# Stick-breaking heads moved into the groups of the other heads of attention 3, and two chunks of the gated linear mixer prepared beside them

## The chip, the cores and the metric

One core of a Trainium2 chip runs the whole program. The metric is the device time in microseconds (us) of one execution, the median of three. The engines are named as in the profile: PE is TensorE, DVE is VectorE, ACT is ScalarE, POOL is GpSimd, and SP issues most DMAs. All data are 32-bit floats. Each matmul instruction of the program stands as two records in the trace, so "x2" behind a matmul row is one instruction.

## The reference, cut to what matters

The program runs three layers on 512 tokens of width 1024. The first two are attention layers with weights of their own and do not change. The third projects its input once and mixes the tokens in three ways, whose outputs are gated, joined and projected back:

```python
# six "NSA" heads, each with three softmax branches: cmp (compressed keys), sel, win
o = gate0 * o_cmp + gate1 * o_sel + gate2 * o_win
# four stick-breaking heads (sb): no softmax, a cumulative sum from the last key back
z = (q @ k.T) * scale                           # keys strictly before the query
log_a = log_sigmoid(z) + reverse_cumsum(log_sigmoid(-z))[next key]
o_sb = exp(log_a) @ v
# six HGRN2 heads (hg): linear attention with a decaying state, in chunks
b = cumsum(log_f);  att = (q * k * exp(b_t - b_s)) summed, causal
o_hg = att @ v + (q * exp(b)) @ state
out = layer_norm(ALPHA * x + concat(o_nsa * silu(z1), o_sb * silu(z2), o_hg * silu(z3)) @ w_out)
```

Tokens are handled in four query tiles of 128 (index i or t, 0 to 3). A tile i sees keys 0 to 128(i+1), so its score rows are 128, 256, 384 or 512 wide; those of the branch cmp are 7, 15, 23 or 31 wide.

## The kernel before

The work around the change is "attention 3", the attention of the third layer, and the mixer stage that follows it, which I call the tail.

**Units.** Attention 3 has 88 units (72 NSA, 16 stick-breaking), each one head of one branch on one query tile, numbered 0 to 87 here in the order of `attention_plan`. Units form groups that share one PSUM bank OB and are closed together: 12 groups of six NSA units (cmp, sel, win of tile 0, then of tile 1, and so on), and then four groups of four stick-breaking units, units 72 to 87. Every engine walks the same list, one step per unit (`steps`). In step r

- PE issues the scores (L919, into SC) of units up to two ahead. For the NSA kinds they come in pairs, at even steps, and the two of a pair have their 64 rows of keys in different halves of the array, because `row_halves` orders heads 0, 3, 1, 4, 2, 5. Then come some filler matmuls (L867), the transposes of unit r's weights (L934, into PT), more fillers, and the products with the values (L897, into OB) of unit r-1.
- DVE first does the cmp mask product of unit r (`finish_weights`, L1677), then masks the new scores (L2023 for NSA, which also finds the row maximum; L1677 for sb), and then what is left over: gates, the closing of the group that ended two steps ago (`finish_group`), and one piece of each open chain.
- ACT does the exponential of each new score row (L1367), a piece of each open chain, copies the transposed weights out of PSUM (L1208, pts<-PT), and then what belongs to finished filler tiles.

**A stick-breaking unit** costs more: DVE adds the mask (L1677), ACT takes abs, exp and log (L1361 to L1363), DVE does a sum, a reversed scan and another sum (L1685, L1975, L1685; `stick_tail`), and ACT a last exp (L1339). Before, its z stands in zm, which has two buffers shared with the other units.

**Fillers.** 25 tiles of input projections (FILLERS[2], eight matmuls each: nz, sbq, sbk, sbvz, hf, hz, hq, hi) are spread over the steps by SPREAD[2]: before, 21 tiles over 68 steps and four over 14 more, so two or three matmuls in each of the steps 0 to 81. A tile `hf` starts a chain of three pieces on DVE and two on ACT (`forget_tile`), one piece a step; its second DVE piece holds the reciprocal of L1893.

**The tail** needs, for each 128-token chunk c, operands made by POOL and ACT: `differences(c)` on POOL, `exponentials(c)` on ACT (L1396 to L1401), `operands(c)` on POOL. Before, POOL starts when the last NSA unit is done and the first stick unit masked, and ACT's part is done inside steps 78 and 84. PE starts the tail when the last group is closed and chunk 0's operands are there; chunk 1's are needed one chunk later. The tail goes on through four chunks, the output projection (L960) and the layer norm.

**Weights** come through a ring of three slots of 2 MB (`ring_slots`), each loaded when the last user of its slot is done.

## Time and profile before

| | us |
|---|---|
| median of three runs (1392.6 to 1395.92) | 1394.83 |
| the profiled execution, whole | 1397.89 |
| its span, first to last instruction | 1396.4 |
| attention 3, first unit to the tail (947.3 to 1256.4) | 309.1 |
| the tail (1256.4 to 1396.4) | 140.0 |
| PE busy over the span | 1232.1 (88%) |
| mean granted clock of PE | 0.917 |

A timeline row gives the start, the length, the engine, the line, what is written from what, the shape, the count, and in brackets how long the engine was idle before it and what ended that. The granted clock is a share of 2.4 GHz; 0.60 in a stretch means that PE ran most of it at 1.2 GHz.

### The profile page before, as it was taken

What the parts mean: (1) busy time and instruction counts of PE and PEld (TensorE: products, weight loads), DVE (VectorE), ACT (ScalarE), POOL (GpSimd) and SP (SyncE); (2) the same over time, 40 slices, a digit from 0 to 9 for tenths busy, and PEclk for the clock granted to TensorE, in tenths of its full rate; (3) what the DMA queues carried; (4) which work ended last, traced back from release to release, by engine and by line L of the source; (5) the groups of instructions that cost most, each with busy time, mean ns of one, the idle gap of its engine ahead of it and who ended that gap; (6) DMA issues with size and microseconds to landing.
All of it is one profiled execution on the core that took longest, in us unless ns stands there. A gap on an engine that the chain in (4) does not pass through costs nothing.

```text
span 1396.4 us, 15111 instructions
## 1 busy us (share of the span) xinstructions
PE 1232.1 (88%) x5264; PEld 687.7 (49%) x5264; DVE 553.4 (40%) x1422; ACT 427.5 (31%) x1086; POOL 112.6 (8%) x140
## 2 busy tenths in 40 slices
PE   4879986999897899889999989999999899867974
PEld 1555453455564444334455555555454556545541
...
GB/s 348 100 91 31 91 121 177 151 211 151 1 1 1 121 61 37 49 97 61 61 61 61 1 0 124 54 186 34 30 36 46 46 61 61 1 0 32 1 31 30
DMA packets 60258, 99.71 MB, mean 71 GB/s; under 512 B 12068, under 2 KB 22129, under 8 KB 60184
## 3 DMA queue, kind: packets, MB, share of 16 engines
...
## 4 chain that ended last, share of the span: by engine, by line
PE 73%; DVE 14%; ACT 6%; DMA 3%; issue 2%; ACTq 1%; POOL 0%; DVEq 0%; SPq 0%; POOLq 0%
PE PR L867 32%; PE OB L897 6%; PE PT L779 6%; PE SC L919 6%; PE PR L779 5%; PE OB L779 4%; PE SC L779 4%; PE PT L934 3%; DMA ring<-in_w_ada 3%; DVE stage L1677 2%; PE PR L960 2%; DVE d L1677 1%; DVE tok L1677 1%; DVE arena L1893 1%; PE PR L851 1%
## 5 line engine op out<-in xcount | busy, mean ns | idle before, releaser
L867 PE MATMUL PR<-ring,hT 128*128 128x512 f32 (+1 forms) x784 | 382.2, 600 | 4.4 <-ACT hT L1208 3.5
L867 PEld LDWEIGHTS PR<-ring,hT 128*128 128x128 f32 x784 | 137.9, 200 | 105.2 <-issue 88.2
L1367 ACT ACTIVATE stage<-stage,nmax 128x256 f32<-128x256 f32 (+7 forms) x200 | 103.7, 519 | 261.3 <-DVE nmax L2023 230.0
L897 PEld LDWEIGHTS OB<-arena,pts 128*128 128x128 f32 (+3 forms) x880 | 132.9, 202 | 99.0 <-issue 76.5
L867 PE MATMUL PR<-hT,ring 128*128 128x512 f32 (+1 forms) x304 | 150.7, 619 | 0.0
L1585 POOL TENSOR_TENSOR arena<-arena 128x192 f32<-128x192 f32 (+1 forms) x118 | 80.4, 681 | 798.0 <-PE OB L897 749.2
L897 PE MATMUL OB<-arena,pts 128*128 128x64 f32 (+4 forms) x880 | 131.0, 278 | 11.4 <-ACT pts L1208 11.4
L919 PE MATMUL SC<-arena 64*128 64x256 f32 (+15 forms) x432 | 114.4, 455 | 10.2 <-DVE nmax L2023 10.2
L934 PEld LDWEIGHTS PT<-ident,stage 128*128 128x128 f32 (+3 forms) x440 | 59.7, 148 | 108.2 <-issue 70.1
L1208 ACT ACTIVATE pts<-PT 128x256 f32<-128x256 f32 (+7 forms) x200 | 80.9, 404 | 95.2 <-PE PT L934 72.8
L934 PE MATMUL PT<-ident,stage 128*128 128x128 f32 (+3 forms) x440 | 88.1, 292 | 20.9 <-ACT stage L1339 11.8
L2023 DVE CUSTOM_DVE_ANT_0 stage<-SC,causal 128x128 f32<-128x128 f32 (+3 forms) x96 | 47.1, 491 | 105.5 <-issue 55.5
L867 PEld LDWEIGHTS PR<-hT,ring 128*128 128x128 f32 (+1 forms) x304 | 51.1, 190 | 52.4 <-issue 51.2
L960 PE MATMUL PR<-ring,hT 128*128 128x512 f32 x128 | 61.3, 632 | 6.1 <-DVE hT L2232 6.1
L2023 DVE CUSTOM_DVE_ANT_0 stage<-SC,arena 128x128 f32<-128x128 f32 (+7 forms) x72 | 27.9, 388 | 81.5 <-PE SC L919 79.8
L919 PEld LDWEIGHTS SC<-arena 64*128 64x128 f32 (+2 forms) x432 | 46.7, 192 | 21.3 <-DVE nmax L2023 10.6
L779 PE MATMUL PR<-ring,hT 128*128 128x512 f32 (+5 forms) x160 | 50.2, 470 | 3.9 <-ACT hT L1251 2.0
L1681 DVE TENSOR_SCALAR t<-PR 128x512 f32<-128x512 f32 (+3 forms) x29 | 17.4, 599 | 87.1 <-PE PR L867 76.2
L779 PE MATMUL SC<-ring,hT 128*128 128x512 f32 (+3 forms) x144 | 51.4, 516 | 0.0
L779 PE MATMUL PT<-ring,hT 128*128 128x512 f32 (+4 forms) x144 | 50.0, 502 | 0.0
L960 PEld LDWEIGHTS PR<-ring,hT 128*128 128x128 f32 x128 | 25.1, 204 | 34.8 <-issue 28.2
L779 PEld LDWEIGHTS PR<-ring,hT 128*128 128x128 f32 x160 | 28.1, 200 | 22.8 <-issue 16.6
...
## 6 DMA issues: line engine op xcount, KB each, us to landing
...
ring<-in_od_w_in SPq DMA_DIRECT2D x8, 2048.0 KB, 14.4
...
ring<-in_ev_w_out SPq DMA_DIRECT2D x2, 2048.0 KB, 10.2
...
```

The costliest lines, as they stand in the source:

```text
L779: mm = pe.matmul(dst, lhs(k), rhs(k), start=(k == 0), stop=(k == K - 1))
L867: mm = pe.matmul(dst, l, r, start=(k == 0), stop=(k == KT - 1))
L897: mm = pe.matmul(ob[:, h * w:h * w + w], pts[0:rows_, v % 2, n * P:n * P + P], vb, start=(n == 0), stop=(n == len(blocks) - 1))
L919: pe.matmul(SC[s % 2][:, 0:n], q, k, start=True, stop=True).then_inc(s_done, 1)
L934: tr = pe.transpose(PT[v % 2][0:w, b * P:b * P + P], pb[:, s % NP, b * P:b * P + w], ident[:, :])
L960: mm = pe.matmul(b[:, :], hT[:, k, i * P:i * P + P], W[:, k, :], start=(k == 0), stop=(k == KT - 1))
L1208: return act.activation(dst, src, ACT.Copy, scale=scale)
L1367: give(act.activation(pb[:, s % NP, 0:n], zm[:, s % 2, 0:n], ACT.Exp, bias=nmax[:, row, c:c + 1], scale=-1.0, accum_out=rsum[:, row, c:c + ...
L1585: return pool.tensor_tensor(dst, a, b, op)
L1677: return dve.tensor_tensor(dst, a, b, op)
L1681: return dve.tensor_scalar(dst, a, s1, None, op0)
L2023: give(dve.tensor_tensor_reduce(out=z, in0=SC[s % 2][:, 0:n], in1=mask, scale=-scale, scalar=start, op0=ALU.add, op1=ALU.min, accum_out=nm ...
```

## The change

- The stick-breaking units no longer form groups of their own. Two of them (heads h and h+1 of tile t) are put into each of eight NSA groups, win of tile 0 to cmp of tile 3 (STICKS), as third and sixth unit of what is then a group of eight. Their products go to columns 384 to 511 of the group's OB, and `finish_group` multiplies them into tok with one more DVE operation.
- "sb" is now among the kinds whose scores are issued in pairs. So a stick unit's scores are paired with those of an NSA unit.
- z and its logs have one buffer each (sbz, sbl) instead of zm and t1/t2, and a semaphore of their own, sb_p. The mask of one stick unit therefore waits for the last exp of the one before. The DVE tail of a stick unit and its last exp are done one step after its mask, behind the copy of the transposed weights on ACT.
- SPREAD[2] is new: 11 tiles over 11 steps (eight matmuls a step), nine over 33 steps (two or three), three over 22 and two over 22 (one or none). The hf tiles end at steps 14, 18 and 21 (before 38, 41 and 44), the last tile at step 87.
- The slot of nz is kept as room for the operands of chunk 0, so that hf, hz, hq, hi and the output weights alternate between the other two slots. POOL makes chunk 0's differences as soon as the three hf chains are done, and chunk 1's when the last stick unit is done (unit 73). ACT's exponentials are cut into three pieces, one a step, behind steps 34 and 79. The rest of the tail's buffers moves within the arena.

The diff, cut to its core:

```diff
-SPREAD = [..., [(21, 68), (4, 14)]]
+SPREAD = [..., [(11, 11), (9, 33), (3, 22), (2, 22)]]
-SIDE_BY_SIDE = ("swa", "cmp", "sel", "win")
+SIDE_BY_SIDE = ("swa", "cmp", "sel", "win", "sb")
+STICKS = dict(zip([(0, "win"), (1, "cmp"), (1, "sel"), (1, "win"), (2, "cmp"), (2, "sel"), (2, "win"), (3, "cmp")],
+                  [(t, h) for t in range(T) for h in (0, 2)]))
...
-            groups += [(kind, i, [[(kind, h, i)] for h in row_halves(NSH)]) for kind in ("cmp", "sel", "win")]
-        groups += [("sb", i, [[("sb", h, i)] for h in range(SBH)]) for i in range(T)]
+            for kind in ("cmp", "sel", "win"):
+                units = [[(kind, h, i)] for h in row_halves(NSH)]
+                if (i, kind) in STICKS:
+                    t, h = STICKS[i, kind]
+                    units[2:2] = [[("sb", h, t)]]
+                    units[5:5] = [[("sb", h + 1, t)]]
+                groups.append((kind, i, units))
...
-HG_EARLY = (78, 84)
+EXP_STEPS = (34, 79)
...
+        sbl = spare[:, 3456:3968]
+        sbz = arena[:, 17088:17600]
...
# ACT, in the loop over the steps
                         if su[0] == "sb":
-                            t = (t1, t2)[s % 2][:, 0:n]
...
-                            stick_tail()
-                            pending.append(s)
+                            link(act.activation(sbl[:, 0:n], sbz[:, 0:n], ACT.Abs))
+                            link(act.activation(sbl[:, 0:n], sbl[:, 0:n], ACT.Exp, scale=-1.0))
+                            say(act.activation(sbl[:, 0:n], sbl[:, 0:n], ACT.Ln, bias=1.0), sb_l, "sb_l")
+                            sticks.append((r_, s))
                             continue
...
                     give(copy(pts[0:r, v % 2, 0:w], PT[v % 2][0:r, 0:w]), pt_ev[v % 2], v // 2 + 1)
+                    if sticks and sticks[0][0] < r_:
+                        stick_tail(sticks.pop(0)[1])
...
-                    if L == 2 and r_ in HG_EARLY:
-                        exponentials(HG_EARLY.index(r_))
+                    if L == 2 and r_ in EXP_STEPS:
+                        chains.append(exponentials(EXP_STEPS.index(r_)))
...
# POOL
-            pool.wait_ge(pv_done, last_v[2, nsa] + 1)
-            pool.wait_ge(masked, s_no["sb", 0, 0])
+            used(pool, ("nz", T - 1))
             differences(0)
             drained(pool, ("hq", 2))
             operands(0)
-            used(pool, ("hi", T - 1))
+            pool.wait_ge(pv_done, s_units[max(sb_no)][3] + 1)
             differences(1)
             operands(1)
...
# DVE
+                    if (i, kind) in STICKS:
+                        t, h = STICKS[i, kind]
+                        dst = tok[:, t, 384 + MN * h:384 + MN * h + P]
+                        link(tt(dst, dst, ob[:, 384:512], ALU.mult))
...
                         if su[0] == "sb":
-                            give(tt(z, SC[s % 2][:, 0:n], mask, ALU.add), masked, s + 1)
-                            stick_tail()
-                            pending.append(s)
+                            if sb_no[s]:
+                                dve.wait_ge(sb_p, sb_no[s])
+                            give(tt(sbz[:, 0:n], SC[s % 2][:, 0:n], mask, ALU.add), masked, s + 1)
+                            sticks.append((r_, s))
                             continue
...
+                    if sticks and sticks[0][0] < r_:
+                        stick_tail(sticks.pop(0)[1])
```

The order of instructions at three places. First PE in the group cmp of tile 3, whose NSA scores are 31 wide. Before, six NSA units with two or three fillers around each (the group's start):

```order
L919 MATMUL SC<-arena 128x31 [waits masked] x2
L867 MATMUL PR<-ring,hT 128x384
L934 MATMUL PT<-ident,stage 31x128 [waits pt_ev0,post]
L867 MATMUL PR<-ring,hT 128x384
L897 MATMUL OB<-arena,pts 128x64 [waits pt_ev1]
L897 MATMUL OB<-arena,pts 128x64 x2
L867 MATMUL PR<-ring,hT 128x384
L934 MATMUL PT<-ident,stage 31x128 [waits pt_ev1,post]
L867 MATMUL PR<-ring,hT 128x384 [waits pr_free1,w_in2]
L867 MATMUL PR<-ring,hT 128x384
```

Now, with two stick units 512 wide in the group:

```order
L942 MATMUL SC<-arena 128x512 [waits masked]
L942 MATMUL SC<-arena 128x31 [waits masked]
L959 MATMUL PT<-ident,stage 31x128 [waits pt_ev0,post]
L888 MATMUL PR<-ring,hT 128x384
L920 MATMUL OB<-arena,pts 128x64 [waits pt_ev1]
L920 MATMUL OB<-arena,pts 128x64 x2
L959 MATMUL PT<-ident,stage 31x128 [waits pt_ev1,post]
L920 MATMUL OB<-arena,pts 128x64 [waits pt_ev0,ob_free]
L942 MATMUL SC<-arena 128x31 [waits masked]
L942 MATMUL SC<-arena 128x512 [waits masked]
L959 MATMUL PT<-ident,stage 128x128 [waits pt_ev0,sb_p]
L959 MATMUL PT<-ident,stage 128x128 x3
```

The scores of a stick unit stand directly before or behind those of an NSA unit, and there is one filler matmul or none between the other steps, where there were two or three. The first `sb_p` is the wait for the group's first stick unit.

Second, DVE at the same place. Before, the first steps of the group, with the closing of the group before it:

```order
L1677 TENSOR_TENSOR stage<-stage,arena 128x31 [waits p_done,pr_free1]
L2023 ISA stage,nmax<-SC,arena 128x31 [waits p_done,s_done,post]
L2023 ISA nmax 128x1
L2023 ISA stage,nmax<-SC,arena 128x31 [waits p_done,s_done,masked]
L2023 ISA nmax 128x1
L1677 TENSOR_TENSOR stage<-stage,arena 128x31 [waits p_done,masked]
L1948 RECIPROCAL fr<-rsum 128x6 [waits pv_done,post]
L1677 TENSOR_TENSOR fr<-fr,arena 128x6 [waits dve_seq]
L1677 TENSOR_TENSOR d<-OB,fr 128x384 [waits dve_seq]
L1677 TENSOR_TENSOR trig<-trig,d 128x384 [waits dve_seq]
L1677 TENSOR_TENSOR tok<-tok,trig 128x384 [waits dve_seq]
```

Now, from the DVE tail of the group's first stick unit to that of its second:

```order
L1708 SCALAR_TENSOR_TENSOR arena<-d,arena 128x512 [waits dve_seq]
L1968 RECIPROCAL fr<-rsum 128x6 [waits pv_done,sb_a]
L1700 TENSOR_TENSOR fr<-fr,arena 128x6 [waits dve_seq]
L1700 TENSOR_TENSOR tok<-tok,OB 128x128 [waits dve_seq]
L1700 TENSOR_TENSOR d<-OB,fr 128x384 [waits dve_seq]
L1700 TENSOR_TENSOR trig<-trig,d 128x384 [waits dve_seq]
L1700 TENSOR_TENSOR tok<-tok,trig 128x384 [waits dve_seq]
L2042 ISA stage,nmax<-SC,arena 128x31 [waits p_done,s_done,ob_free]
L2042 ISA nmax 128x1
L1700 TENSOR_TENSOR arena<-SC,causal 128x512 [waits sb_p,s_done,masked]
L1700 TENSOR_TENSOR stage<-stage,arena 128x31 [waits p_done,masked]
L1708 SCALAR_TENSOR_TENSOR d<-arena,ring 128x512 [waits sb_l,post]
```

The closing of win of tile 2 (five operations, now six) stands between the tail of the first stick unit and the masks of the next pair, and the cmp product of a later unit behind the stick's mask.

Third, DVE at the chain of hf tile 1. Before, between 384-wide masks:

```order
L2023 ISA stage,nmax<-SC,arena 128x384 [waits p_done,s_done,hg_b]
L2023 ISA nmax 128x1
L2023 ISA stage,nmax<-SC,arena 128x384 [waits p_done,s_done,masked]
L2023 ISA nmax 128x1
L1681 TENSOR_SCALAR arena<-arena 128x512 [waits hg_a,masked]
L1893 RECIPROCAL arena<-arena 128x512 [waits dve_seq]
L1685 SCALAR_TENSOR_TENSOR arena<-arena 128x512 [waits dve_seq]
L1682 TENSOR_SCALAR d<-arena 128x512 [waits dve_seq]
L1685 SCALAR_TENSOR_TENSOR arena<-arena,d 128x512 [waits dve_seq]
L1685 SCALAR_TENSOR_TENSOR d<-arena 128x512 [waits hg_a,hg_b]
L1905 SCALAR_TENSOR_TENSOR arena<-d 128x128 [waits dve_seq] x4
```

Now, in the group cmp of tile 1, with the mask of a stick unit ahead of it, and a cmp product and a stick tail behind it:

```order
L1700 TENSOR_TENSOR arena<-SC,causal 128x128 [waits sb_p,s_done,post]
L2042 ISA stage,nmax<-SC,arena 128x15 [waits p_done,s_done,masked]
L2042 ISA nmax 128x1
L1704 TENSOR_SCALAR arena<-arena 128x512 [waits hg_a,masked]
L1916 RECIPROCAL arena<-arena 128x512 [waits dve_seq]
L1708 SCALAR_TENSOR_TENSOR arena<-arena 128x512 [waits dve_seq]
L1705 TENSOR_SCALAR d<-arena 128x512 [waits dve_seq]
L1708 SCALAR_TENSOR_TENSOR arena<-arena,d 128x512 [waits dve_seq]
L1700 TENSOR_TENSOR stage<-stage,arena 128x15 [waits p_done,hg_b]
L1708 SCALAR_TENSOR_TENSOR d<-arena,ring 128x128 [waits sb_l,post]
L1996 SCALAR_TENSOR_TENSOR d<-d 128x128 [waits dve_seq]
L1708 SCALAR_TENSOR_TENSOR arena<-d,arena 128x128 [waits dve_seq]
```

The chain's block (clamp, reciprocal, three more) is the same and stands behind the masks of the same step as before; in front of the next step's masks there is now also the work of the stick units and, right behind these rows, the closing of win of tile 0.

## Rows read from the trace of the kernel before

**Rows 1.** Windows: busy time (instructions), granted clock, DMA by stretch of attention 3

```profile
core 0: us, PE busy (x) PEld busy (x) DVE busy (x) ACT busy (x) POOL busy (x), PEclk, DMA share, GB/s
...
1062.00:1112.00 50.00, 41.38 (x152) 22.33 (x151) 34.64 (x63) 23.87 (x51) 0.00 (x0) 0.86 0.10 32
1112.00:1186.00 74.00, 74.00 (x347) 45.33 (x348) 22.92 (x73) 33.07 (x81) 0.00 (x0) 1.00 0.16 58
1186.00:1224.00 38.00, 33.76 (x120) 19.74 (x119) 27.92 (x50) 24.62 (x54) 20.05 (x30) 0.87 0.00 1
1224.00:1256.40 32.40, 21.07 (x81) 15.07 (x81) 17.89 (x23) 17.66 (x27) 25.61 (x33) 0.60 0.00 0
947.30:1256.40 309.10, 284.86 (x1124) 162.09 (x1125) 136.71 (x349) 144.45 (x362) 45.67 (x62) 0.91 0.10 35
```

**Rows 2.** Timeline of PE, three idle stretches: start, us, what, [idle before]

```profile
1070.63 0.41 PE L934 MATMUL PT<-ident,stage 128*23 128x128 f32 x1 [3.02 <-DVE stage L1677]
...
1214.07 0.90 PE L934 MATMUL PT<-ident,stage 128*128 128x128 f32 x3 [2.34 <-ACT stage L1339]
...
1245.42 1.11 PE L934 MATMUL PT<-ident,stage 128*128 128x128 f32 x4 [4.38 <-ACT stage L1339]
```

**Rows 3.** Timeline of PE, win of tile 3 with fillers, then a single stick score

```profile
1171.77 1.13 PE L919 MATMUL SC<-arena 64*128 64x512 f32 x4
1172.83 0.91 PE L867 MATMUL PR<-ring,hT 128*128 128x384 f32 x2
1173.58 0.60 PE L934 MATMUL PT<-ident,stage 128*128 128x128 f32 x4
1174.02 0.81 PE L867 MATMUL PR<-ring,hT 128*128 128x384 f32 x2
1174.67 1.00 PE L897 MATMUL OB<-arena,pts 128*128 128x64 f32 x8
1175.50 0.86 PE L867 MATMUL PR<-ring,hT 128*128 128x384 f32 x2
...
1224.00 1.12 PE L919 MATMUL SC<-arena 64*128 64x512 f32 x2
```

**Rows 4.** Timeline of DVE, the forget chain and the closing of a win group

```profile
1065.10 3.35 DVE L1893 RECIPROCAL arena<-arena 128x512 f32<-128x512 f32 x1
...
1069.67 0.69 DVE L1685 SCALAR_TENSOR_TENSOR arena<-arena,d 128x512 f32<-128x512 f32 x1
...
1125.70 0.19 DVE L1948 RECIPROCAL fr<-rsum 128x6 f32<-128x6 f32 x1 [1.51 <-PE OB L897]
...
1127.31 0.56 DVE L1677 TENSOR_TENSOR tok<-tok,trig 128x384 f32<-128x384 f32 x1
```

**Rows 5.** Timeline of all engines, stick units 512 wide

```profile
1238.40 0.69 DVE L1677 TENSOR_TENSOR stage<-SC,causal 128x512 f32<-128x512 f32 x1 [0.85 <-ACT stage L1339]
...
1239.86 1.22 DVE L1975 TENSOR_TENSOR_SCAN d<-d 128x512 f32<-128x512 f32 x1
...
1242.76 0.63 ACT L1361 ACTIVATE t<-stage 128x512 f32<-128x512 f32 x1
...
1245.63 1.59 DVE L1975 TENSOR_TENSOR_SCAN d<-d 128x512 f32<-128x512 f32 x1
```

**Rows 6.** ACT by form, exps and copies of units 512 wide: xcount | busy, mean ns | idle

```profile
L1367 ACT ACTIVATE stage<-stage,nmax 128x512 f32<-128x512 f32 x12 | 8.7, 722 | 18.8 <-DVE nmax L2023 18.6
...
L1208 ACT ACTIVATE pts<-PT 128x512 f32<-128x512 f32 x16 | 9.6, 597 | 8.2 <-PE PT L934 7.9
```

**Rows 7.** Timeline of PE, a cmp unit of tile 3

```profile
1127.62 0.43 PE L897 MATMUL OB<-arena,pts 31*128 31x64 f32 x2
1127.98 0.41 PE L919 MATMUL SC<-arena 64*128 64x31 f32 x4
```

**Rows 8.** Timeline of POOL, differences of chunk 0 and operands of chunk 1

```profile
1188.28 10.22 POOL L1585 TENSOR_TENSOR arena<-arena 128x192 f32<-128x192 f32 x15 [749.16 <-PE OB L897]
...
1242.87 11.07 POOL L1585 TENSOR_TENSOR arena<-arena 128x192 f32<-128x192 f32 x14 [4.04 <-ACT arena L1401]
```

118 lines of the change are left out of this document (60 added, 58 removed).

## The prediction

> **What bounds the kernel now.** I read the page's slices first: PE is at nine tenths or more in most of the span, with dips around 1066 to 1110 us and from 1186 us to the end. Then the windows of attention 3, because only that stage is reordered [rows 1]. Over its 309.1 us PE is busy 284.86. From 1112 to 1186 us, NSA units with two or three fillers each, it is busy all the time at full clock. Three stretches lose time. In 1062 to 1112, where the forget chains run, PE is idle 50.00 - 41.38 = 8.6 us at a granted clock of 0.86. In 1186 to 1224, the first stick units, 38.00 - 33.76 = 4.2 us at 0.87. In 1224 to 1256.4, stick units without fillers, 32.40 - 21.07 = 11.3 us at 0.60. The timeline names what PE waited for: DVE's cmp product behind a forget chain (3.02 us), and ACT's last stick exp (2.34 and 4.38) [rows 2]. Busy time at a lower clock is also lost. The reader can take it as busy time x (1 - granted clock): 41.38 x 0.14 = 5.8, 33.76 x 0.13 = 4.4, 21.07 x 0.40 = 8.4, together 18.6 us. So attention 3 holds 24.2 us of idleness and 18.6 us of slow clock, 42.8 us in all, and 309.1 - 42.8 = 266.3 us of PE work that stays (with about 3 us of slow start, which both kernels have). 42.8 us is the most that the change can win there; the question is how much of it comes back.
>
> **Durations used.** 512 wide, from start to start [rows 3]: a score pair 1.06 us, a filler 384 wide 0.65 (0.75 behind a score), the transposes 0.44, the value products 0.83. A cmp unit's value products take 0.36, a cmp pair of scores about 0.33 [rows 7], its one transpose about 0.11, a quarter of the four. On DVE a mask of a stick unit takes 0.69, its tail 2.7 (0.69, a scan of 1.22, 0.69 and gaps), on ACT each step 0.63, so abs, exp and log 2.0 [rows 5]. An NSA exp is 0.72 plus the read of its sum, 0.9 in all, and a copy 0.60 [rows 6]. The forget chain's DVE block is 1065.10 to 1070.36 and the clamp before it, 5.8 us; the closing of a win group 1125.70 to 1127.87, 2.2, with the new stick product 2.5 [rows 4].
>
> **Part 1, scores.** A single stick score takes 1224.00's 1.12 us, as long as a pair's 1.13 [rows 3]: two scores in different halves of the array cost one. The change's pairs are (stick h, head 1), both in rows 0 to 63, and (head 4, stick h+1), both in rows 64 to 127. So they run one behind the other, and heads 1 and 4, which shared a slot, no longer do. That is one more slot in each of eight groups, in proportion to the width: 0.42 (128), 0.33 (cmp) three times, 0.63 (256) twice, 0.84 (384) twice: +4.3 us. The Trainium skill (TensorEngine Tiling (Array Packing), Theoretical Speedup) gives up to twofold for a contraction of 64 rows; it would be had only if the two lay in different halves, which the change's name for the kind ("side by side") suggests. By it the sum would be 4.3 us lower; the rows of a half decide, and I keep +4.3.
>
> **Part 2, fillers.** The same 200 matmuls. Before they stand in two pieces in 82 steps (some 162 pieces), now in some 128. A piece costs about 0.1 us to get into (0.75 against 0.65) [rows 3]: -3 us.
>
> **Part 3, forget chains.** They come at steps 14 to 24 instead of 38 to 47, in groups 128 and 15 wide. Before, a step was about 3.8 us of PE work, now about 2.4 (two fillers of 0.86 to 0.94, and 0.6). The chain is as long as it was: DVE block 5.8, then ACT's exp and log 1.3 and the copy, before PE can do that step's value products. Chain 0 (step 16): ready 0.4 (scores) + 0.7 (masks) + 5.8 + 1.3 + 0.3 = 8.5 us after the step begins; PE's own work to there is 5.2: stall 3.3. Chain 1 (step 20): the cmp product of unit 21 stands behind the block, at 7.3; PE is there at 3.8: 3.5. Chain 2 (steps 23, 24): DVE comes to it late, behind chain 1's scan pieces 2.6, the closing of win of tile 0 2.5 and a stick tail 1.1; I count 2.1 + 1.0 + 4.4 + 0.5 = 8. In all 15 us idle, and 3.5 us of slow clock behind it (the granted clock fell to 0.86 in the window of the chains before, with idle stretches like the 3.02 us one [rows 1, 2]; the next wait hides part of it). 18.5 us, where the same chains cost 8.6 + 5.8 = 14.4 before. Bounds: 12 (chains 1 and 2 hide each other) to 27.
>
> **Part 4, stick units in their groups.** Worked through for cmp of tile 3 (units 68 to 75), from the issue of the first stick score. Score 1.1, mask 1.8, logs 3.85, exp and copy of the first unit 4.6, DVE tail 6.55, last exp 7.25. PE's own work to that transpose: scores 1.3, two steps of 0.1 + 0.65 + value products 0.83 and 0.36, scores 1.3: 4.4. So PE waits 2.8 us (first for the copy, then for sb_p). Then DVE closes win of tile 2, 2.5 us, until 9.15, and only then masks the next pair; the second stick unit's mask ends at 10.1, its logs at 12.1, and ACT's copy of the first stick unit's weights stands behind them: 12.75. PE wants it at 9.4 to 9.5. The cmp product of unit 72 stands on DVE behind the second tail, 15.0. PE reaches the sixth unit at 16.6 where its own work makes 9.2: 7.1 us lost. For cmp of tile 2 (384 wide, closing of win of tile 1) the same steps end at 14.25 against 9.95: 4.3. For sel and win of tile 2 the NSA matmuls are long, and only ACT's copies are late: 2.0 and 2.6. The four groups of tiles 0 and 1 have two fillers a step, 6.5 us of PE work against 3 to 4.5 of chain: 0. Sum 16 us. Bounds: 4 (if PE, slowed, hides most of it) to 26.
>
> **Part 5, the last units.** In sel and win of tile 3 a pair has one or two fillers. ACT needs 2.8 us to begin its second exp, 3.7 to end it, and 4.35 for the copy, with its own and DVE's durations above; PE wants the copy at 2.8 + 0.65 per filler. That is 0.8 us for each of three pairs with one filler. With ACT's operand exps (4 us over three steps at 34 and 79, each in steps of 2.2 to 2.7 us) I take 3 us (0 to 8). Slow clock behind parts 4 and 5: 3 us (0 to 8). At the end the last group's closing, 2.2 us, stands before PE may start the tail, where a stick group's was 0.4: +1.7.
>
> **Part 6, the tail.** Chunk 1's operands are ready at about 1256 us, as the tail starts, and chunk 0's before them; POOL needs 10.2 us for differences, and for operands 11.07 us for 14 of the 16 operations, so 13 [rows 8]. Earlier preparation wins nothing. After unit 73 there are 14 steps of 2.2 to 2.7 us, over 30 us, for chunk 1's 10.2 + 4 + 13 us; that hides it, since it is wanted only one chunk into the tail. If it slips, it costs up to 3 us. I take 0. The output weights' second half is loaded at the end of attention 3 and is wanted nearly 30 us later: 0.
>
> **Sum.** 266.3 + 4.3 - 3 + 18.5 + 16 + 3 + 3 + 1.7 = 309.8 us against 309.1: +0.7 us. On the profiled execution's own 1397.89 us that is 1398.6; this execution lies 3.1 us above the median 1394.83, so about 1395.5, and I put down 1395. In other words all that the sticks' stage gives back (4.2 + 4.4 + 11.3 + 8.4 = 28.3 us) is spent on thinner cover elsewhere.
>
> **Rivals.**
> Rival A, faster: the chains hide. PE at the lower clock needs twice as long for its own work, so stalls shrink; parts 3 to 5 together would cost 26 instead of 42 us. For it speaks that 1112 to 1186 has no idleness at all; against it that the cover was then two to three fillers. 1395.5 - 16 = about 1380; with half of it, 1388.
> Rival B, slower: one mechanism, the forget chains in steps 14 to 30. Their DVE work (three times 9.6 us, with masks, stick tails and closings some 41 us) exceeds PE's 25 us there. If DVE and ACT hand over to each other without overlap, the stretch is 15 us longer than PE's work instead of 18.5 with slow clock, and PE stays at 1.2 GHz until step 35: +11, 1406. It decides from 20 us of PE idleness between steps 14 and 26.
> Rival C, POOL beside DVE. A scan beside POOL takes 1.59 us, without it 1.22 [rows 5]; I took 1.22. Three tails of tile 2 now meet operands(0), where all of tile 2's and 3's met POOL before, so this is at most 1 us either way. The Trainium skill (SBUF — State Buffer, SBUF: two separate sides) says the port shared by the two engines is an exclusive lock held for a whole instruction. Should each of nine two-input operations of those tails lose one POOL instruction (10.22 us / 15 = 0.68 us), DVE would be 6 us late, half of it hidden: 1398.
> Rival D, the change does not do what it says: a stick unit is still done alone, with PE waiting for each sb_p. Then the stick stage's old 28.3 us is lost inside the groups, in place of part 4's 16 and its 3 us of slow clock: +9, 1405.
>
> **Chances.** Forecast (1391 to 1399) 0.38; rival A with its half way 0.36; B 0.16; C 0.05; D 0.05. A difference under about 0.2%, 2.8 us, can't be told from none. The forecast's own range gives half to "same"; faster gets A and a little of it, 0.40; same 0.24; slower 0.36. Range 1378 to 1407: it holds rival A and rival B at their full size, and leaves out that the chains hide altogether or that several costs reach their upper bounds together.
>
> **What would show it.** Right: the stage from the last stick unit to the tail has no PE idleness over 1 us; PE idle about 15 us in the forget chains, a stall of over 2 us in cmp of tile 3 with ACT's copy named; a score beside a stick unit not shorter than the sum of two; attention 3 still about 310 us and the tail 140. Wrong: a mean clock above 0.97 in attention 3, or less than 20 us of PE idleness there, means faster; a tail shorter by over 2 us would mean that operands did bound it.

## The result, and the profile after

The changed kernel takes 1409.04 us (median of four runs, 1406.09 to 1412.78) against 1393.82 us of the kernel before on the same chip: ratio 1.0106, 95% interval 1.0088 to 1.0124. It is 15 us slower. The prediction was 1395 us with a range of 1378 to 1407; the time lies 2 us above the range. Slower had been given 0.36.

The profiled execution took 1408.91 us, 11.0 us more than that of before. Attention 3 begins at 944.6 us (947.3 before) and ends at 1267.9, so it lasts 323.3 us where it was 309.1: 14.2 us more. The tail from there to the span's end is 139.5 us, 140.0 before. All of the loss is inside attention 3, and the windows show where. The columns are those of [rows 1].

```profile
core 0: us, PE busy (x) PEld busy (x) DVE busy (x) ACT busy (x) POOL busy (x), PEclk, DMA share, GB/s
944.60:1029.00 84.40, 83.97 (x238) 40.79 (x238) 13.32 (x53) 21.58 (x65) 0.00 (x0) 0.96 0.07 23
1029.00:1100.00 71.00, 58.00 (x193) 30.31 (x193) 47.89 (x111) 34.67 (x96) 8.09 (x15) 0.86 0.12 41
1100.00:1119.00 19.00, 18.35 (x84) 11.53 (x84) 8.60 (x25) 14.43 (x33) 0.00 (x0) 1.00 0.24 78
1119.00:1158.00 39.00, 36.09 (x141) 19.81 (x142) 14.94 (x48) 18.43 (x52) 0.00 (x0) 0.91 0.01 3
1158.00:1203.00 45.00, 40.14 (x213) 26.57 (x211) 23.61 (x52) 25.29 (x57) 12.69 (x16) 0.96 0.13 47
1203.00:1230.00 27.00, 21.78 (x81) 12.72 (x82) 12.26 (x32) 11.12 (x28) 2.10 (x5) 0.75 0.00 1
1230.00:1268.00 38.00, 30.78 (x180) 21.55 (x179) 13.28 (x36) 19.21 (x37) 16.80 (x27) 0.91 0.08 26
944.60:1268.00 323.40, 289.11 (x1125) 163.28 (x1126) 133.89 (x353) 144.73 (x364) 39.69 (x62) 0.91 0.09 30
```

The rows are: the first steps, the forget chains, the end of tile 1, cmp of tile 2, sel and win of tile 2, cmp of tile 3, sel and win of tile 3. Read as in the prediction, idleness is length less busy, and slow clock is busy x (1 - granted clock):

| stretch | idle | slow clock | predicted idle | predicted slow |
|---|---|---|---|---|
| 944.6 to 1029 | 0.4 | 3.4 | 0 | 3 |
| 1029 to 1100, forget chains | 13.0 | 8.1 | 15 | 3.5 |
| 1100 to 1119 | 0.7 | 0 | 0 | 0 |
| 1119 to 1230, sticks in tiles 2 and 3 | 13.0 | 10.2 | 16 | 3 for both rows |
| 1230 to 1268, last units | 7.2 | 2.8 | 3 + 1.7 | |
| sum | 34.3 | 24.5 | 35.7 | 9.5 |

Over all of attention 3, PE's work at full rate is then 289.11 - 24.5 = 264.6 us. In before it was 284.86 - 22.0 = 262.9 us (with 3.4 us of slow start), so scores and pieces cost 1.7 us; +1.3 was predicted. The clock is given to 0.01, so a sum over 290 us is known to about 1 us and no better. The idleness came out 1.4 us smaller than predicted, the slow clock 15.0 us larger; the whole miss in attention 3 was 323.3 - 309.8 = 13.5 us.

Idle stretches of PE in the forget chains and in cmp of tile 3 (start, us, what, idle before and what ended it), which answer to [rows 2]:

```profile
1048.75 0.69 PE L920 MATMUL OB<-arena,pts 128*128 128x64 f32 x2 [4.20 <-ACT pts L1233]
1063.01 0.28 PE L959 MATMUL PT<-ident,stage 128*15 128x128 f32 x1 [3.39 <-DVE stage L1700]
1079.02 0.40 PE L959 MATMUL PT<-ident,stage 128*15 128x128 f32 x1 [4.12 <-DVE stage L1700]
...
1207.73 0.40 PE L920 MATMUL OB<-arena,pts 31*128 31x64 f32 x2 [1.98 <-ACT pts L1233]
1210.39 1.07 PE L959 MATMUL PT<-ident,stage 128*128 128x128 f32 x4 [0.98 <-ACT stage L1363]
1215.85 1.10 PE L920 MATMUL OB<-arena,pts 128*128 128x64 f32 x8 [1.28 <-ACT pts L1233]
1218.22 0.42 PE L959 MATMUL PT<-ident,stage 128*31 128x128 f32 x1 [0.93 <-DVE stage L1700]
```

And cmp of tile 3 on all engines, the group that the prediction worked through, from the issue of its first stick score at 1202.89:

```profile
1202.89 1.26 PE L942 MATMUL SC<-arena 64*128 64x512 f32 x4
1204.11 0.69 DVE L1700 TENSOR_TENSOR arena<-SC,causal 128x512 f32<-128x512 f32 x1 [2.93 <-PE SC L942]
1206.22 0.63 ACT L1382 ACTIVATE ring<-ring 128x512 f32<-128x512 f32 x1
1207.32 0.56 ACT L1233 ACTIVATE pts<-PT 31x128 f32<-31x128 f32 x2
1208.93 0.69 DVE L1708 SCALAR_TENSOR_TENSOR arena<-d,arena 128x512 f32<-128x512 f32 x1
1209.70 0.63 ACT L1363 ACTIVATE stage<-arena 128x512 f32<-128x512 f32 x1 [1.81 <-DVE arena L1708]
1211.59 0.56 DVE L1700 TENSOR_TENSOR tok<-tok,trig 128x384 f32<-128x384 f32 x1
1212.43 0.69 DVE L1700 TENSOR_TENSOR arena<-SC,causal 128x512 f32<-128x512 f32 x1
1214.54 0.63 ACT L1382 ACTIVATE ring<-ring 128x512 f32<-128x512 f32 x1
1215.20 0.90 ACT L1233 ACTIVATE pts<-PT 128x512 f32<-128x512 f32 x2
1217.97 0.19 DVE L1700 TENSOR_TENSOR stage<-stage,arena 128x31 f32<-128x31 f32 x1
1218.43 1.49 PE L888 MATMUL PR<-ring,hT 128*128 128x384 f32 x2
```

Counted from 1202.89, the mask ends at 1.9 us (1.8 predicted), the logs at 4.0 (3.85), the tail at 6.7 (6.55), the last exp at 7.4 (7.25), the closing of win of tile 2 at 9.3 (9.15), the second mask at 10.2 (10.1), its logs at 12.3 (12.1), and the cmp product of unit 72 begins at 15.1 (15.0). The order of waits in the prediction was right to 0.2 us. What it lacked stands in the last row: two fillers take 1.49 us in one record where they take 0.81 at full clock [rows 3].

### The profile page after: what moved, and what is told of

It reads as the page before. It is cut to its first block, busy times and chain, and to the rows that moved or that the text cites. A ratio compares the mean times of both kernels' runs of the same rounds, so it can differ in the third digit from the quotient of the medians.

```text
span 1407.4 us, 15111 instructions
## 1 busy us (share of the span) xinstructions
PE 1233.7 (88%) x5264; PEld 688.5 (49%) x5264; DVE 550.2 (39%) x1426; ACT 428.2 (30%) x1090; POOL 107.0 (8%) x140
## 4 chain that ended last, share of the span: by engine, by line
PE 69%; DVE 15%; ACT 7%; issue 3%; DMA 3%; ACTq 1%; POOL 0%; DVEq 0%; SPq 0%; POOLq 0%
PE PR L888 29%; PE PT L800 6%; PE SC L942 5%; PE OB L920 5%; PE PR L800 4%; PE OB L800 4%; PE SC L800 4%; DMA ring<-in_w_ada 3%; PE PT L959 3%; DVE stage L1700 2%; PE PR L985 2%; DVE d L1700 2%; DVE arena L1708 1%; DVE tok L1700 1%; ACT stage L1387 1%
## 5 line engine op out<-in xcount | busy, mean ns | idle before, releaser
L888 PE MATMUL PR<-ring,hT 128*128 128x512 f32 (+1 forms) x784 | 378.3, 600 | 4.4 <-ACT hT L1233 3.5
L888 PEld LDWEIGHTS PR<-ring,hT 128*128 128x128 f32 x784 | 141.1, 202 | 107.7 <-issue 90.0
L920 PEld LDWEIGHTS OB<-arena,pts 128*128 128x128 f32 (+4 forms) x880 | 129.8, 199 | 115.1 <-issue 83.6
L920 PE MATMUL OB<-arena,pts 128*128 128x64 f32 (+5 forms) x880 | 129.9, 276 | 21.9 <-ACT pts L1233 21.9
L942 PE MATMUL SC<-arena 64*128 64x256 f32 (+15 forms) x432 | 115.3, 458 | 10.9 <-DVE nmax L2042 10.2
L959 PEld LDWEIGHTS PT<-ident,stage 128*128 128x128 f32 (+4 forms) x440 | 58.2, 149 | 98.8 <-issue 67.8
L959 PE MATMUL PT<-ident,stage 128*128 128x128 f32 (+4 forms) x440 | 89.4, 295 | 17.8 <-DVE stage L1700 9.2
L1610 POOL TENSOR_TENSOR ring<-arena 128x192 f32<-128x192 f32 (+1 forms) x30 | 17.6, 585 | 664.8 <-DVE arena L1928 646.4
L1610 POOL TENSOR_TENSOR arena<-arena 128x192 f32<-128x192 f32 (+2 forms) x66 | 48.5, 735 | 130.1 <-PE OB L920 55.5
L1253 ACT ACTIVATE t<-t 128x512 f32<-128x512 f32 (+3 forms) x32 | 16.8, 525 | 91.1 <-DVE t L1704 91.1
## 6 DMA issues: line engine op xcount, KB each, us to landing
ring<-in_od_w_in SPq DMA_DIRECT2D x8, 2048.0 KB, 14.4
ring<-in_ev_w_out SPq DMA_DIRECT2D x2, 2048.0 KB, 10.2
```

What stands on the lines that cost most here:

```text
L888: mm = pe.matmul(dst, l, r, start=(k == 0), stop=(k == KT - 1))
L920: mm = pe.matmul(ob[:, h * w:h * w + w], pts[0:rows_, v % 2, n * P:n * P + P], vb, start=(n == 0), stop=(n == len(blocks) - 1))
L942: pe.matmul(SC[s % 2][:, 0:n], q, k, start=True, stop=True).then_inc(s_done, 1)
L959: tr = pe.transpose(PT[v % 2][0:w, b * P:b * P + P], pb[:, s % NP, b * P:b * P + w], ident[:, :])
L1610: return pool.tensor_tensor(dst, a, b, op)
```

## The experiments

Each ratio is against runs of the kernel before on the same chip; "of before" is left out below. One per cent is 13.9 us.

**Theory after reading the traces.** The stick chains in the groups of tiles 2 and 3 make the new stalls (part 4's mechanism), and the slow clock behind the stalls, which the prediction took at a third of its size (6.5 us for 21.1), is what carried the time out of the range. Rivals: (a) PE's own work, the scores that run one behind the other; (b) DVE and ACT set the pace, so that the clock costs nothing; (c) the forget chains, which now stand under thinner steps.

**filled_after and filled_before.** Matmuls that nobody reads, ahead of PE's waits, into the bank or columns that PE owns at that moment:

```diff
+                    for _ in range(FILL_T.get(r, 0)):
+                        pe.matmul(PT[v % 2][:, 0:P], ident[:, :], ident[:, :], start=True, stop=True)
                     pe.wait_ge(post, post_no[v] + 1)   # and sb_p, p_done
...
+                    for _ in range(FILL_V.get(r, 0)):
+                        pe.matmul(ob[:, h * w:h * w + w], ident[:, :], ident[:, 0:w], start=True, stop=True)
                     pe.wait_ge(pt_ev[v % 2], v // 2 + 1)
...
```

> The changed kernel, with matmuls whose results nobody uses put ahead of the waits at which PE stood idle in attention 3 (steps 17, 21, 24, 38 and the waits in the groups of tiles 2 and 3), each somewhat shorter in sum than the wait. Theory 1 (what the prediction missed is the slow clock behind the many new stalls: 24.5 us in attention 3 by busy time x (1 - granted clock), of which 21 us behind stalls): the granted clock stays near 1.00, and a good half of the 21 us comes back, 1409 - 11 = 1398 us; the rest turns into longer waits. Rival (DVE and ACT set the pace in those groups, and a faster PE only waits longer): within 2 us of 1409. Third possibility: the added matmuls delay DVE's or ACT's work and it gets slower, 1412.

> The kernel before, with unused matmuls ahead of PE's waits in steps 41, 45, 48, 75, 76, 80, 83 to 86 of attention 3. Theory 1 (slow clock behind stalls is worth its whole size): of 18.6 us at least half comes back, 1394 - 9 = 1385 us. Rival (the stick units at the end are set by DVE and ACT, so that a fast PE only waits longer): the part behind the forget chains comes back alone, 3 to 5 us, 1390.

Measured: filled_after 1415.29 us, 1.0139 (1.0116 to 1.0162); filled_before 1409.22 us, 1.0099 (1.0079 to 1.0119). Both slower, since the fill was twice what I meant:

```profile
1047.34 8.15 PE L921 MATMUL OB<-ident 128*128 128x64 f32 x72
...
1063.77 5.52 PE L957 MATMUL PT<-ident 128*128 128x128 f32 x48
```

36 and 24 matmuls stand as 72 and 48 records of 0.11 us. As a test of the price they were a miss; they did show that a filled wait keeps the clock up. They were repeated with half the counts.

> The changed kernel with unused matmuls ahead of PE's waits as before, but half as many of them. In the first try each of them went through the array in two pieces of 0.11 us, so they took 8.15 us where the wait had been 4.20, and 5.52 and 7.31 us where it had been 3.39 and 4.12; the slow clock behind the stalls of steps 12 to 87 was gone (0.0 us of it left), and the time still rose by 4 us because the surplus delayed PE. Now they fill 33 us, a little less than the waits. Theory 1 (slow clock behind the stalls counts in full): of about 20 us half or more comes back, 1409 - 12 = 1397 us. Rival (DVE and ACT set the pace around each stall, a fast PE waits longer): 1407 to 1409.

> The kernel before with half as many unused matmuls ahead of PE's waits (24 us of them in steps 41, 45, 48, 75, 76, 80, 83 to 86; the first try had put 10.27 us where PE had stood 4.38). Theory 1: about half of the 18.6 us of slow clock comes back, 1394 - 8 = 1386 us. Rival (DVE and ACT set the pace): 1392 to 1394; the stick units at the end above all, where PE works 12.7 us at full rate in 32.4.

Measured: filled2_after 1398.38 us, 1.0013 (0.9999 to 1.0027), 0.93 points under the changed kernel, 13 us, as theory 1 asked (1397); attention 3 in its trace is 9.1 us shorter. Windows of the forget chains, of the rest and of the whole of attention 3:

```profile
1028.00:1098.00 70.00, 65.24 (x302) 41.94 (x301) 48.09 (x111) 35.04 (x95) 8.10 (x15) 0.95 0.11 38
1098.00:1257.20 159.20, 152.69 (x876) 107.16 (x875) 71.94 (x190) 88.34 (x204) 31.46 (x47) 1.00 0.09 30
943.00:1257.20 314.20, 302.11 (x1414) 190.10 (x1414) 133.67 (x355) 145.09 (x364) 39.56 (x62) 0.98 0.09 31
```

The busy times now hold the unused matmuls too. Slow clock fell from 24.5 to 302.11 x 0.02 = 6.0 us, and attention 3 from 323.3 to 314.2. The stretch of the forget chains hardly moved (71.0 to 70.0 us): PE does not set the pace there, and rival (b) holds; that DVE does is borne out by norecip_after below. Behind 1098 us, 168.0 us became 159.2: there the clock had a price. filled2_before took 1396.62 us, 1.0013 (1.0000 to 1.0027): no gain, the rival. Counted from the start of attention 3, its stick row 1239.67 below comes 297.3 us in, where 1245.42 of before [rows 2] came at 298.1. Three rows of filled2_before show why so little was won:

```profile
1229.50 0.60 ACT L1217 ACTIVATE pts<-PT 128x512 f32<-128x512 f32 x1
1233.18 2.45 ACT L1405 ACTIVATE arena<-arena 128x2688 f32<-128x2688 f32 x1 [3.08 <-POOL ring L1594]
1239.67 1.11 PE L943 MATMUL PT<-ident,stage 128*128 128x128 f32 x4 [3.84 <-ACT stage L1348]
```

ACT has come to chunk 1's exponentials (step 84) and waits 3.08 us for POOL's differences, with the last stick units queued behind; a faster PE only arrives there earlier. The fill of step 86, after it, was too long and cost 2.6 us more (from the row 1239.67 to the next value products 6.8 us, 4.1 in before), so that this run bounds the gain at the end from below only. Attention 3 was 310.8 us long here, 308.2 without that excess, against 309.1.

**halves.** The two sticks of a group exchange places, for rival (a):

```diff
-                    units[2:2] = [[("sb", h, t)]]
-                    units[5:5] = [[("sb", h + 1, t)]]
+                    units[2:2] = [[("sb", h + 1, t)]]
+                    units[5:5] = [[("sb", h, t)]]
...
```

> The changed kernel with the two stick heads of each group in exchanged places, so that the score pairs (stick h+1, head 1) and (head 4, stick h) lie in different row halves of the array. Nothing else is changed. Theory 1 (part 1 of the prediction: two scores in the same half run one behind the other, and cost one slot more in each of eight groups): pairs beside a stick fall from the sum of two to the time of one, 4.3 us of PE work go, and attention 3 becomes 4 us shorter, so about 1405 us. Rival: where sticks stand in tiles 2 and 3, DVE and ACT set the pace, and PE only waits longer; then only the groups of tiles 0 and 1 give anything: 1 to 1.5 us, so 1408.

Measured: 1405.30 us, 1.0067 (1.0048 to 1.0086), 5 us less than the changed kernel (the intervals just miss each other), and attention 3 is 4.0 us shorter. The scores of a stick unit 512 wide with those of an NSA unit 384 wide, in the changed kernel

```profile
1179.27 1.77 PE L942 MATMUL SC<-arena 64*128 64x512 f32 x4
1180.97 0.55 PE L959 MATMUL PT<-ident,stage 128*128 128x128 f32 x3
```

and the same pair with the sticks exchanged:

```profile
1179.38 1.12 PE L942 MATMUL SC<-arena 64*128 64x512 f32 x4
1180.43 0.55 PE L959 MATMUL PT<-ident,stage 128*128 128x128 f32 x3
```

From start to start 1.70 us became 1.05, the time of the wider one alone. Part 1's 4.3 us are confirmed. The Trainium skill (TensorEngine Tiling (Array Packing), Theoretical Speedup) promises up to twofold for a contraction of 64 rows, and the trace agrees once the two lie in different halves (1.70 to 1.05 us, 1.6 times). It is a third of the loss, and it had been counted: not the cause of the miss.

**norecip_after and norecip_before.** The forget chains' price, for rival (c):

```diff
-                link(dve.reciprocal(key, key))
```

The key is then left uninverted.

> The changed kernel without DVE's reciprocal in the forget chain (3.35 us in each of three chains; the forget gate's key is then left uninverted, a changed computation). Theory 1 (each chain stalls PE for as long as it is late, part 3): the three stalls of 4.20, 3.39 and 4.12 us shrink by 3.35 each, 10 us, and 8.1 us of slow clock behind them fall to 2: 1409 - 14 = 1395 us. Rival (the chains' stalls hide other lateness of DVE and ACT in steps 14 to 25, which then takes their place): only 5 us, 1404.

> The kernel before without DVE's reciprocal in the forget chain, as done to the changed kernel, which it made 7.7 us faster (1.0106 to 1.0051 of before). If the chains' stalls in before (3.02, 3.41 and 2.19 us, and 5.8 us of slow clock) go wholly, which theory 1 asks for since each is shorter than 3.35 us: 1394 - 12 = 1382 us. Rival (other lateness takes their place, as it did in the changed kernel, where idleness in steps 14 to 25 fell only from 13 to 6 us): 1388.

Measured: norecip_after 1402.42 us, 1.0051 (1.0033 to 1.0069), so 0.55 points or 7.7 us less; norecip_before 1382.89 us, 0.9899 (0.9879 to 0.9920), 14 us less. In before the three stalls (3.02, 3.41 and 2.19 us) shrink to nothing, 0.59 and 0.51 us. In the changed kernel others stand in their place:

```profile
1043.50 0.43 PE L920 MATMUL OB<-arena,pts 128*128 128x64 f32 x2 [0.83 <-ACT pts L1233]
1051.50 0.43 PE L920 MATMUL OB<-arena,pts 128*128 128x64 f32 x2 [0.42 <-ACT pts L1233]
1053.84 0.28 PE L959 MATMUL PT<-ident,stage 128*15 128x128 f32 x1 [1.00 <-DVE stage L1700]
1061.97 0.39 PE L959 MATMUL PT<-ident,stage 128*15 128x128 f32 x1 [2.33 <-DVE stage L1700]
```

Without the reciprocals the changed kernel is further behind its counterpart (1.52 points) than with them (1.06). So the distance does not come from the reciprocals' meeting thin steps; rival (c) holds only in this form: under the chains lies other lateness (masks, stick tails, closings), some 6 us of idleness and 3 of slow clock, that the old order did not have. The stretch itself became 11 us shorter (70.6 to 59.6), so DVE's operations did set its length; behind it 2 us were lost again.

**late_forget.** The hf tiles behind the hz tiles, which moves the chains to steps 29 to 40:

```diff
+     (("w", "hz"), [("hz", i) for i in range(T)]),
      (("w", "hf"), [("hf", m) for m in range(3)]),
-     (("w", "hz"), [("hz", i) for i in range(T)]),
-EXP_STEPS = (34, 79)
+EXP_STEPS = (46, 79)
```

> The changed kernel with the forget projections (hf) behind the gate projections (hz) in the list of fillers, so that the three forget chains run at steps 29 to 40, in the groups sel and win of tile 1 (256 keys wide), in place of steps 14 to 25 (128 and 15 wide); ACT's exponentials of chunk 0 move from step 34 to 46. Theory 1 (a chain stalls PE by what its step lacks in PE work, part 3): a step there has 3.1 to 3.3 us of PE work against 2.4, so three chains over two steps each lose some 4 us less idleness and 3 us less slow clock: 1402 us. Rival (DVE is as full there, with the stick tails 256 wide, so that the chains stall as before or more): 1409 or above.

Measured: 1405.83 us, 1.0074 (1.0055 to 1.0093), 4.5 us less where 7 were expected, and the intervals overlap. Its stalls are 2.93, 4.57 and 3.58 us, all named as ACT's copy: wider steps, and the same kind of wait.

**short_after and short_before.** The stick chain cut short in both kernels (here after; before alike):

```diff
-  link(act.activation(sbl[:, 0:n], sbz[:, 0:n], ACT.Abs))
-  link(act.activation(sbl[:, 0:n], sbl[:, 0:n], ACT.Exp, scale=-1.0))
-  say(act.activation(sbl[:, 0:n], sbl[:, 0:n], ACT.Ln, bias=1.0), sb_l, "sb_l")
+  say(act.activation(sbl[:, 0:n], sbz[:, 0:n], ACT.Abs), sb_l, "sb_l")
...
-  link(stt(d1[:, 0:n], z, 0.0, l, ALU.max, ALU.add))
-  link(dve.tensor_tensor_scan(...))
-  say(stt(z, d2[:, 0:n], -1.0, z, ALU.mult, ALU.add), sb_a, "sb_a")
+  say(stt(z, l, -1.0, z, ALU.mult, ALU.add), sb_a, "sb_a")
```

This leaves out most of the function.

> The changed kernel with the stick-breaking chain cut short: ACT computes only the first of its three functions before DVE's tail, and the tail only its last operation, without the scan (computation changed). A stick unit's way from mask to weights is some 3.3 us shorter at 512 wide (two ACT functions of 0.63, DVE 0.69 and 1.22), ACT and DVE have that much less to do in each of 16 units. Theory 1 (part 4: in the groups of tiles 2 and 3 PE waits because ACT and DVE are kept by the stick chains; 20.2 us of idleness and 13.0 of slow clock in steps 38 to 87): two thirds of what lies in the four stick groups goes, 1409 - 14 = 1395 us. Rival (the NSA units' own exp and copy and the closings set the pace there, with or without sticks): -3 to -5 us, 1405.

> The kernel before with the same cut in the stick chain. The stick units at its end (1186 to 1256.4 us, 15.5 us idle, 12.8 us of slow clock) are bounded by this chain in either theory. About 3 us less in each of the last six units, hidden in part: 1394 - 14 = 1380 us. If it gains as much as the changed kernel, the sticks' cost was moved and not lowered; if the changed kernel gains more, sticks in the groups cost more than sticks at the end.

Measured: short_after 1385.45 us, 0.9934 (0.9916 to 0.9951), 24 us under the changed kernel; short_before 1382.83 us, 0.9924 (0.9906 to 0.9941), 10.6 us under before. With short chains the two orders take the same time, within 1.4 us; shortening gave the changed kernel 13 us more than it gave before. In the groups cmp of tile 2 to cmp of tile 3, and over attention 3, short_after shows

```profile
1118.00:1202.00 84.00, 82.33 (x419) 51.56 (x417) 32.90 (x107) 43.02 (x113) 13.07 (x20) 1.00 0.08 26
942.30:1240.50 298.20, 277.10 (x1124) 158.90 (x1124) 111.71 (x321) 129.68 (x332) 38.13 (x62) 0.94 0.10 32
```

The same stretch between two pairs of scores, first in the changed kernel and then in short_after:

```profile
1124.25 0.70 PE L942 MATMUL SC<-arena 64*128 64x256 f32 x4
1228.59 1.13 PE L942 MATMUL SC<-arena 64*128 64x512 f32 x4
...
1119.82 0.70 PE L942 MATMUL SC<-arena 64*128 64x256 f32 x4
1201.30 1.13 PE L942 MATMUL SC<-arena 64*128 64x512 f32 x4
```

104.3 us became 81.5: 22.8 of the 25.1 us by which attention 3 shrank lie here. They answer to the ledger: 13.0 idle and 10.2 slow clock in 1119 to 1230. This settles that the stick chains make the loss in these groups. It does not settle the comparison with before, for in short_before ACT waits longer still for POOL, at the place seen above:

```profile
1228.17 2.44 ACT L1394 ACTIVATE arena<-arena 128x2688 f32<-128x2688 f32 x1 [7.11 <-POOL ring L1583]
...
1233.33 1.12 PE L934 MATMUL PT<-ident,stage 128*128 128x128 f32 x4 [11.06 <-ACT stage L1339]
```

so that some 7 us of what shorter chains give are lost there (PE's wait was 4.38 us in before). How much of the 13 us is the sticks' dearer place in groups, and how much this wait of the old order, the two runs do not separate.

**short_act, noscan and copy_first.** Whose share is it? short_act makes only the ACT edit above; noscan leaves out only the scan; copy_first keeps the computation and moves ACT's copy:

```diff
+                    late = L == 2 and r_ and any(s_units[s][2][0] == "sb" for s in new)
+                    if late:
+                        copy_out(r_, v, sus)
                     for s in new:
...
```

> The changed kernel with only ACT's part of the stick chain cut: the first of its three functions alone, DVE's tail whole (computation changed). 1.05 us less at 384 wide and 1.26 at 512, on the path to the weights and ahead of ACT's copy of another unit's weights. If ACT's queue is what PE waits for (theory 1: 15 of the 22 rows of PE's idleness name ACT's copy): 15 of the 24 us that the whole cut gave, 1409 - 15 = 1394 us. If it is only the length of the chain, 1.26 of 3.2 us, two fifths: -9 us, 1400.

> The changed kernel without the scan in DVE's tail of a stick unit (1.22 us at 512 wide, computation changed), ACT's part whole. If only the length of the chain counts: -9 us, 1400, as with ACT's part cut. If ACT's queue is the bound: -3 us, 1406.

> The changed kernel with ACT's copy of the weights put ahead of the stick unit's three functions in the eight steps that issue a stick score (and the other step), computation unchanged. Theory 1 (the copies are late because they stand behind 1.9 us of functions): the stalls that name the copy in steps 45 to 85 (18 us with their slow clock in groups with sticks) halve, while the stick chain begins up to 1 us later: 1409 - 6 = 1403 us. Rival (the stick's weights are as late as the copy, and the one wait takes the place of the other): 1409 or slower, up to 1413.

Measured: short_act 1394.79 us, 0.9995 (0.9983 to 1.0007), 15 us less; noscan 1399.20 us, 1.0031 (1.0018 to 1.0045), 10.5 us less. Per us of chain taken away (1.26 and about 1.25 at 512 wide) ACT's share is worth more, perhaps as its queue also holds the copies; but DVE's counts two thirds as much, which "ACT's queue alone" (-3) excludes. Together they make the 24 us (15 and 10.5). copy_first took 1427.14 us, 1.0226 (1.0212 to 1.0240), 17 us more than the changed kernel, and beyond what the rival had allowed. The wait only changes its name and grows:

```profile
1225.67 1.09 PE L959 MATMUL PT<-ident,stage 128*128 128x128 f32 x4 [3.00 <-ACT stage L1363]
1233.50 0.42 PE L959 MATMUL PT<-ident,stage 128*31 128x128 f32 x1 [2.50 <-DVE stage L1707]
```

ACT now waits for PE's transposes before it begins the stick's functions. The rows that named the copy had not shown a queue in the wrong order, but a chain that PE, ACT and DVE pass around.

**reversed and reversed_all.** The widest sticks in the first groups, where each step has two or three fillers:

```diff
-                  [(t, h) for t in range(T) for h in (0, 2)]))
+                  [(t, h) for t in reversed(range(T)) for h in (0, 2)]))
...
```

> The changed kernel with the sticks given to the groups in the opposite order of tiles: the two pairs of tile 3 (512 wide) in win of tile 0 and cmp of tile 1, those of tile 2 in sel and win of tile 1, those of tile 1 in cmp and sel of tile 2, those of tile 0 (128 wide) in win of tile 2 and cmp of tile 3. Computation unchanged. Theory 1 (what costs is a long stick chain where a step has one filler or none): in steps 44 to 75 a chain is 0.4 to 2.8 us shorter, so most of the 24 us that the cut chain gave comes back there, 16 us, and in steps 14 to 27, where the forget chains run, longer stick scores give PE 6 us more to do and DVE 6 us more: cost 0 to 8 us. Sum 1409 - 12 = 1397 us. Rival (the early part is bounded by DVE, which has 9.6 us per forget chain there already): 1403 to 1409.

> The same order, with the forget key on ACT and the two sticks of a group in exchanged places. Exchanged places gave 0.4% alone; the key on ACT gave 11 us in the kernel before and nothing in the changed one, where sticks kept ACT in the same steps. Theory 1: with the widest sticks in those steps DVE is the fuller engine, so the key on ACT gives 3 us and the exchange 5: 1389 us, under the kernel before. Rival (ACT, with 3 functions for each wide stick and 5 for each forget chain, becomes the bound there): no better than reversed.

Measured: reversed 1411.76 us, 1.0118 (1.0100 to 1.0136), the same as the changed kernel: theory 1 was wrong here. Its first and second part:

```profile
1031.00:1118.00 87.00, 69.71 (x229) 37.05 (x229) 56.21 (x110) 41.51 (x94) 8.10 (x15) 0.82 0.09 32
1118.00:1272.50 154.50, 140.47 (x657) 87.00 (x657) 63.71 (x191) 81.56 (x206) 30.47 (x47) 0.90 0.09 31
```

Idleness and slow clock in the forget stretch rose from 21.1 to 17.3 + 12.5 = 29.8 us, and behind it they fell from 33.9 to 28.1 us, where theory 1 had asked for 16 less. What was saved was lost again: a wide stick beside a forget chain costs as much as beside thin steps. reversed_all took 1398.50 us, 1.0029 (1.0015 to 1.0044): the key on ACT and the exchange give 12 us here, more than the 5 us that the exchange gave alone, which speaks for DVE's load in that stretch; no run separates the two in this order. It is not under before.

**act_before, act_halves and act_late_exp.** The exact form of what norecip tried: 1/(1+exp f) as exp(-ln(1+exp f)) on ACT, behind the output that DVE waits for.

```diff
-  if n == 0:
-      link(act.activation(key, key, ACT.Exp))
   link(act.activation(u, u, ACT.Exp))
   say(act.activation(u, u, ACT.Ln, bias=1.0), hg_a, "hg_a")
+  if n == 0:
+      link(act.activation(key, key, ACT.Exp))
+      link(act.activation(key, key, ACT.Ln, bias=1.0))
+      link(act.activation(key, key, ACT.Exp, scale=-1.0))
...
-                link(ts(key, key, 1.0, ALU.add))
-                link(dve.reciprocal(key, key))
```

act_late_exp also has `HG_EARLY = (78, 87)`.

> The kernel before with the forget key 1/(1+exp f) computed on ACT as exp(-ln(1+exp f)) behind the other output of that step, in place of DVE's addition and its reciprocal of 3.35 us: the same function, and off the chain that PE waits for. Theory 1: as without the reciprocal (0.9899 of before), less up to 2 us for two more ACT functions of 0.63 us in each of three chains: 1383 to 1385 us. Rival (ACT's exps behind it stall PE instead): 1388 or more.

> The changed kernel with both the forget key on ACT and the two sticks of a group in exchanged places. Theory 1: the two gains add up, 0.55% (reciprocal left out) less 1 us for ACT and 0.4% (exchanged places), together about -12 us: 1397. Rival (both act on the same stalls): 1401.

> The kernel before with the forget key on ACT (0.9921 of before) and, besides, ACT's exponentials for chunk 1 behind the last stick unit (step 87) in place of step 84, where they hold ACT for 4 us while PE waits for the last stick's weights (4.38 us). Theory: 3 us more, 1394 x 0.9921 - 3 = 1380 us. Rival (chunk 1's operands then come late in the tail): no gain, 1383, or slower.

Measured: act_before 1381.55 us, 0.9921 (0.9902 to 0.9939), 11 us under before and 26 under the changed kernel: with act_late_exp the fastest exact version of this study. In its trace the window that was 39.38 busy of 48.00 at 0.87 in before (1062 to 1110) reads

```profile
1062.00:1110.00 48.00, 45.67 (x205) 26.68 (x205) 27.11 (x70) 33.53 (x72) 0.00 (x0) 1.00 0.10 33
```

act_halves took 1402.17 us, 1.0064 (1.0043 to 1.0086), no better than halves by the ratio (1.0067), though its forget stretch is 64 us long instead of 70; attention 3 is 3 us shorter than in halves (316.1 against 319.3), so how much the key on ACT is worth there stays open between nothing and 6 us. act_late_exp, 1384.12 us, 0.9920 (0.9905 to 0.9936), gave nothing more: the rival. Its attention 3 is 4.0 us shorter than that of act_before, and its tail 4.2 us longer (145.0 against 140.8), which fits late operands of chunk 1.

## Why the prediction was wrong, point by point

**What bounds the kernel now.** The three stretches were read rightly, but "42.8 us is the most that the change can win" put slow clock and idleness in one purse. filled2_before took some 10 us of that slow clock away up to the end (18.6 to 7.9 by its windows) and was not faster, 2.6 us of it owing to the fill itself: PE was waiting on DVE, on ACT and, from step 84, on POOL.

**Part 1, scores, and part 2, fillers.** Right as far as can be told: +1.7 us of PE work together where +1.3 was said, and halves gives the part 1 share back. Part 2's -3 us has no run of its own.

**Part 3, forget chains.** The stalls were 4.20, 3.39 and 4.12 + 0.50 us where 3.3, 3.5 and 8 were worked out, with small ones 13.0 us of idleness against 15. The third was taken twice too large. The slow clock was 8.1 us where 3.5 was taken, though [rows 1] had 5.8 beside 8.6 idle. The sum, 21.1, lies inside the bounds of 12 to 27. But filled2_after shows that this clock is nearly free (1 us came back), as DVE sets the pace (norecip_after); [rows 4] are its longest operations.

**Part 4, sticks in their groups.** The mechanism was right, in cmp of tile 3 step by step to 0.2 us, and the idleness 13.0 us where 16 was said. short_after shows that cutting these chains short gives 23 us back here, idleness and slow clock together. That they alone make the difference between the two orders is not shown: by the same ledger the forget chains went from 14.4 us in before to 21.1, and the sticks with the last units from 28.3 to 33.2.

**Part 5, the failed step.** "Slow clock behind parts 4 and 5: 3 us (0 to 8)" measured 10.2 + 2.8 = 13.0 us, 5 us above its upper bound, and filled2_after gave 8.8 us of attention 3 back behind 1098 us, so it was time and not only a reading. The number had no row behind it, while [rows 1] had two: 4.2 us idle with 4.4 slow, 11.3 with 8.4. By that ratio of 12.8 to 15.5 the 20.7 us of idleness would have carried 17 us instead of 3, and the forecast would have been about 1409. That it meets the result is partly luck: the idleness of these stretches carried 13.0 us and not 17, 0.6 us for each, and the rest of the gap was the forget chains'. The last units cost 7.2 us idle, not 3 + 1.7: the pair in step 81 alone waits 2.25 us, and the closing 2.5.

The Trainium skill (TensorE: Matmul & The Clock Gate, What's actually happening) says that the default state is throttled and that activity releases it. The trace agrees: 0.75 in the stretch of cmp of tile 3, and 1.00 behind 1098 us when the same waits are filled. The same page of the Trainium skill (Terms) prices the loss as the time at the low clock times the lost share; by that, as an estimate, filled2_before should have won some 10 us, and it won none, nor more than 1 in attention 3 when the fill's own 2.6 us are taken off. The measurement decides: in this kernel the price came back only behind 1098 us of the changed order, and not where PE waits for DVE, ACT and POOL anyway.

**Part 6.** The tail is as long as before: right. That earlier preparation wins nothing was not the whole of it for the order before, where POOL's differences and operands [rows 8] held ACT in step 84 as soon as the sticks became faster; in the changed kernel this wait is gone, a gain that the text did not name and that counts only once the sticks are faster.

**Rivals.** The result lies nearest to B's number (1406), but not for its reason: PE idleness between steps 14 and 26 was 12.2 us, not the 20 from which B was to decide. A failed: parts 3 to 5 cost 55 us where A had 26 and the sum 42; a slower PE did not shorten the waits by much (33.9 us of them where 35.7 were counted). C came to little: two scans 384 wide took 1.23 us beside POOL and 0.96 without it, 0.3 us each. D was wrong in mechanism (PE does not wait for each sb_p alone), though its 1405 was near.

**What would show it.** A stall of over 2 us in cmp of tile 3 was announced; it came in pieces of 1.98, 0.98, 1.28 and 0.93 us, with ACT's copy named in two. The serial scores, the tail and the idleness in the chains came as said, attention 3 did not. That PE would not stand idle for over 1 us between the last stick unit and the tail was wrong: it did for 1.16, 2.25 and 2.51 us.
